# Expert outputs of a pair side by side: one 0/1 product over 128 slots for two over 64, and the expert stage of a hybrid encoder layer reordered by pairs of experts

## The reference, cut to what matters

```python
def _hier_moe(h, router_group, router_expert, e_gate, e_up, e_down):
    ...
    combine = jnp.sum(jax.nn.one_hot(expert_ids, N_EXPERTS, dtype=f32) * w_top[..., None], axis=1).astype(h.dtype)
    out = jnp.zeros_like(ht)
    for e in range(N_EXPERTS):
        hid = jax.nn.silu(ht @ e_gate[e]) * (ht @ e_up[e])
        out = out + combine[:, e:e + 1] * (hid @ e_down[e])
    return out.reshape(B, T, D)

def _layer(...):
    ...
    x = x + gt2 * _hier_moe(h2, router_group, router_expert, expert_w_gate, expert_w_up, expert_w_down)
```

## Time and profile before

| | us |
|---|---|
| median of three runs | 1513.69 (1513.60 to 1515.83) |
| the profiled execution, device time | 1509.26 |
| its span in the profile | 1507.5 |
| TensorE busy in the span | 1400.7 (93%) |
| weights' queue (q1), share of 16 engines' span | 49.8%, 285.07 MB |

### The profile page before, as it was taken

How to read it: one execution, slowest core, us unless ns; L and a number is a source line. 1 busy time by engine, 2 the same in 40 slices (tenths; PEclk the granted TensorE clock), 3 DMA queues, 4 the chain that set the end, 5 groups by cost and what they waited for, 6 DMA issues and landing times. The chain is left out here.

```text
span 1507.5 us, 31643 instructions
## 1 busy us (share of the span) xinstructions
PE 1400.7 (93%) x14017; PEld 1015.6 (67%) x14017; DVE 722.2 (48%) x1184; ACT 473.9 (31%) x764; POOL 167.2 (11%) x200
## 2 busy tenths in 40 slices
PE   5899999999999998888879999799999999999986
PEld 1778999999998987777779998653333333333332
DVE  3322134652235456556555666624555554554545
ACT  2333345554554543333335442110100110011002
POOL 2000000010112124324201101000000000000000
PEclk9999999999999998999999999789999999999988
DMA  8656422234432210000422461499999999999951
GB/s 313 195 187 222 139 72 71 83 110 130 124 90 60 68 44 11 4 5 4 135 56 74 163 213 63 198 407 426 427 426 427 425 427 426 427 426 425 426 232 61
DMA packets 124510, 310.01 MB, mean 206 GB/s; under 512 B 12407, under 2 KB 97617, under 8 KB 109010
## 3 DMA queue, kind: packets, MB, share of 16 engines
q1 hardware_dynamic: 113680, 285.07, 49.8%
q10 hardware_dynamic: 7522, 15.57, 2.9%
q0 software_dynamic: 3168, 7.30, 1.3%
HBM read 299.06 MB, written 12.79 MB: 207 GB/s over the span
## 5 line engine op out<-in xcount | busy, mean ns | idle before, releaser
L838 PE MATMUL bank<-upper2end 128*128 128x272 f32 x3168 | 419.2, 291 | 5.4 <-DVE upper2end L1079 5.4
L838 PEld LDWEIGHTS bank<-upper2end 128*128 128x128 f32 x3168 | 403.4, 189 | 27.5 <-issue 26.2
L1056 DVE TENSOR_TENSOR upper2end<-upper,upper2end 128x1024 fp32r<-128x1024 f32 x66 | 81.7, 1238 | 286.3 <-ACT upper2end L604 286.2
L2711 PE MATMUL bank<-upper7b 128*64 128x512 f32 x784 | 208.0, 603 | 1.0 <-DVE upper7b L3058 1.0
L2491 ACT ACTIVATE upper_r7b<-lower 128x512 fp32r<-128x512 f32 x30 | 18.9, 629 | 407.4 <-DVE lower L3084 407.4
L3111 DVE TENSOR_TENSOR lower<-lower,bank 128x1024 f32<-128x1024 f32 (+1 forms) x75 | 91.4, 1218 | 97.2 <-PE bank L2689 97.2
L2711 PEld LDWEIGHTS bank<-upper7b 128*64 128x64 f32 x784 | 57.7, 137 | 96.9 <-issue 93.0
L2689 PEld LDWEIGHTS bank<-upper_r7b 64*128 64x128 f32 x600 | 52.5, 191 | 86.5 <-DVE lower L3111 58.6
L2689 PE MATMUL bank<-upper_r7b 64*128 64x512 f32 x600 | 93.2, 430 | 18.0 <-DVE lower L3111 9.6
L2543 PE MATMUL bank<-upper_r 128*128 128x272 f32 x768 | 103.0, 294 | 3.2 <-DVE upper_r L2958 3.2
L2543 PEld LDWEIGHTS bank<-upper_r 128*128 128x128 f32 x768 | 99.4, 191 | 5.9 <-DVE upper_r L2790 3.6
(11 more groups left out here) (412 smaller groups left out, 1904.0 us busy)
## 6 DMA issues: line engine op xcount, KB each, us to landing
upper7b<-in_expert_w_gate SPq DMA_DIRECT2D x25, 2048.0 KB, 20.3
upper7b<-in_expert_w_up SPq DMA_DIRECT2D x24, 2048.0 KB, 21.9
upper7b<-in_expert_w_down SPq DMA_DIRECT2D x23, 2048.0 KB, 17.0
upper<-in_w_in SPq DMA_DIRECT2D x66, 512.0 KB, 3.9
lower<-in_w_ada SPq DMA_DIRECT2D x23, 1024.0 KB, 5.0
lower<-in_expert_w_down SPq DMA_DIRECT2D x9, 2048.0 KB, 16.3
lower<-in_expert_w_up SPq DMA_DIRECT2D x8, 2048.0 KB, 23.3
lower<-in_expert_w_gate SPq DMA_DIRECT2D x7, 2048.0 KB, 20.8
```

The costliest lines, as they stand in the source:

```text
L838: m = mm(psum[s][:, c, 0:HALF], w_part[s][:, k, :], h_part[:, k, c * HALF:(c + 1) * HALF], start=k == 0 and w_part is w_high and h_part is ...
L1056: ve.tensor_tensor(w_rest[u % 2], w_slot[u % 2], w_high[u % 2].bitcast(F32), ALU.subtract).then_inc(w_split, 1)
L2711: m = nc.tensor.matmul(psum[s][64 * b:64 * b + 64, 1, :], x_t[(e // 2) % 2][:, k, s * BLK:(s + 1) * BLK], w[:, k, :], start=k == 0, stop=k ...
```

## The change

Both experts of a pair get their `down` in one call: the two experts stand in the two column halves of the array, over four blocks `f` and two output halves `b`, and fill both banks of `psum[2]` with 128 slots by 1024. So scale, rounding and rest become one instruction of 1024 columns for a pair in place of two of 512, and a tile of rows takes 2 parts x 2 halves = 4 products that contract over 128 partitions. The 0/1 matrix is one of 128 slots by 544 rows for a pair; its last 96 columns are zeroed once.

The order on TensorE becomes, for pair p: `gate_up(2p)` with tiles 0 and 1 of pair p - 1 before step 6; `gate_up(2p + 1)` with the turning of expert 2p and tiles 2 and 3 before step 3; `rows_turned(p + 1)`; the turning of expert 2p + 1; tile 4; `down(p)`. `STREAM` takes the matching order. PSUM is dealt anew: gate and up results in banks 0 and 2, turned results in bank 3, turned rows in banks 6 and 7, tiles in `psum[2]`, `psum[3]`, `psum[2]`, `psum[3]`, `psum[0]`. The transposed rows have one buffer, not two. The modulation's gate rows are fetched in full width to all 128 partitions, 2 x 512 KB in place of 4 x 128 KB. The last pair's outputs are now split as all others, by halves of 512. The turning of the first pair's rows, in banks 6 and 7, now waits until the code rows have been copied out of these banks (`code_out`).

```diff
-        act_g = low.take(4, BLK)
-        hid = low.take(4, BLK)
-        gu = [Region(pos_oh_at + 512 * s).take(512) for s in range(2)]
+        hid = [low.take(4, BLK) for _ in range(2)]
...
-        oh_t = moe_r.take(2, 5, P)
-        y_parts = [[moe_r.take(512) for _ in range(2)] for _ in range(2)]
...
+        oh_t = moe_r.take(5 * P)
+        y_parts = [moe_r.take(D) for _ in range(2)]
...
-        STREAM = [("gate", 0), ("up", 0)]
-        for e in range(NE):
-            STREAM += [("gate", e + 1), ("up", e + 1)] * (e + 1 < NE) + [("down", e)]
+        STREAM = []
+        for e in range(0, NE, 2):
+            STREAM += [("gate", e), ("up", e), ("gate", e + 1), ("up", e + 1), ("down", e), ("down", e + 1)]
...
+        GU_BANK = (bank(0), bank(2))
+        TURNED = bank(3)
+        X_BANK = (bank(6), bank(7))
+        ADD_BANKS = (2, 3, 2, 3, 0)
+        LAST_BANKS = (0, 3, 1, 2, 0)
...
+                    sp.dma_start(gt2_b[:, s, :], mod_dram[s, 5 * D:6 * D].partition_broadcast(P)
+                                 ).then_inc(last_rows_in, 16)
...
+                    coef_of_prompt(r, 0)
+                    for p in range(NP):
+                        silu(r, 2 * p)
+                        silu(r, 2 * p + 1)
+                        if p < P_LAST:
+                            y_rounded(r, p)
+                            coef_of_prompt(r, p + 1)
+                    for b in range(2):
+                        last_rounded(r, b)
...
+                    if p == 0 and first(r):
+                        pe.wait_ge(code_out, 4)
...
+                        if h == 0 and p >= 2:
+                            pe.wait_ge(moe_added, r * ADDS + (5 * p - 6))
...
+                    pe.wait_ge(*landed(r, "gate", e))
+                    pe.wait_ge(*landed(r, "up", e))
...
-                    elif not first(r):
...
+                        if s == 0 and p >= 2:
+                            pe.wait_ge(moe_added, r * ADDS + (5 * p - 5))
...
+                        if s == 0 and k == 6 and p:
+                            rows_added(r, p - 1, 0)
+                            rows_added(r, p - 1, 1)
+                        if s == 1 and k == 3:
+                            turned(r, e - 1)
+                            if p:
+                                rows_added(r, p - 1, 2)
+                                rows_added(r, p - 1, 3)
                         for b, w in enumerate(gate_and_up):
...
+                def down(r, p):
+                    pe.wait_ge(hid_done, r * NE + (2 * p + 2))
+                    for s in range(2):
+                        pe.wait_ge(*landed(r, "down", 2 * p + s))
+                    if p:
+                        pe.wait_ge(moe_added, r * ADDS + (5 * p - 2))
+                    w = [weights_of("down", 2 * p + s) for s in range(2)]
                     for f in range(4):
                         for b in range(2):
...
+                            for s in range(2):
+                                m = nc.tensor.matmul(psum[2][64 * s:64 * s + 64, b, :], hid[s][:, f, :],
+                                                     w[s][:, f, b * 512:(b + 1) * 512], start=f == 0, stop=f == 3)
                     m.then_inc(dn_mm, 1)
...
+                def rows_added(r, p, j):
+                    if j == 0:
+                        pe.wait_ge(yrest_done, r * Y_STEPS + (p + 1))
+                        pe.wait_ge(oh_done, r * NP + (p + 1))
+                    if j == 1:
+                        pe.wait_ge(x_t9, r * NE + (2 * p + 4))
+                    if j in (2, 3):
+                        pe.wait_ge(moe_added, r * ADDS + (5 * p + j - 1))
+                    if j == 4:
+                        pe.wait_ge(gu_out, r * NE + (2 * p + 3))
+                    out = psum[ADD_BANKS[j]]
+                    for part in range(2):
+                        for b in range(2):
+                            m = nc.tensor.matmul(out[:, b, :], oh_t[:, j * P:(j + 1) * P],
+                                                 y_parts[part][:, b * 512:(b + 1) * 512], start=part == 0,
+                                                 stop=part == 1)
+                    m.then_inc(moe_mm, 1)
...
+                def last_rows_added(r, j):
+                    if j == 0:
+                        pe.wait_ge(oh_done, r * NP + NP)
+                        pe.wait_ge(moe_added, r * ADDS + ADDS)
                     if j == 4:
                         pe.wait_ge(x3_done, r * 5 + 1)
...
+                    for part, ready in enumerate((yh_done, yrest_done)):
+                        for b in range(2):
+                            if j == 0:
+                                pe.wait_ge(ready, r * Y_STEPS + (P_LAST + b + 1))
+                            m = nc.tensor.matmul(psum[LAST_BANKS[j]][:, b, :], oh_t[:, j * P:(j + 1) * P],
+                                                 y_parts[part][:, b * 512:(b + 1) * 512], start=part == 0,
+                                                 stop=part == 1)
+                    m.then_inc(last_mm, 1)
...
+                    for p in range(NP):
+                        gate_up(r, 2 * p)
+                        gate_up(r, 2 * p + 1)
+                        if p < P_LAST:
+                            rows_turned(r, p + 1)
+                        turned(r, 2 * p + 1)
+                        if p:
+                            rows_added(r, p - 1, 4)
+                        down(r, p)
+                    for j in range(5):
+                        last_rows_added(r, j)
...
+                        ve.memset(oh_t[:, T:5 * P].bitcast(F32), 0.0).then_inc(oh_pad, 1)
+                        v.wait_ge(oh_pad, 1)
...
+                    ve.tensor_scalar(oh_t[:, 0:T], code_rows[0], tgt[:, p:p + 1], None, ALU.is_equal).then_inc(oh_half, 1)
+                    v.wait_ge(oh_half, r * NP + (p + 1))
+                    ve.scalar_tensor_tensor(out=oh_t[:, 0:T], in0=code_rows[1], scalar=tgt[:, p:p + 1],
+                                            in1=oh_t[:, 0:T].bitcast(F32), op0=ALU.is_equal, op1=ALU.add
+                                            ).then_inc(oh_done, 1)
...
+                def down_scaled(r, p):
+                    v.wait_ge(dn_mm, r * NP + (p + 1))
+                    v.wait_ge(coef_done, r * NP + (p + 1))
+                    ve.tensor_tensor(y_full, psum[2].rearrange("t b c -> t (b c)"), coef, ALU.mult).then_inc(y_done, 1)
+                    v.wait_ge(yh_done, r * Y_STEPS + (p + 1))
+                    ve.tensor_tensor(y_parts[1], y_full, y_parts[0].bitcast(F32), ALU.subtract).then_inc(yrest_done, 1)
+
+                def last_scaled(r):
+                    v.wait_ge(dn_mm, r * NP + NP)
+                    v.wait_ge(coef_done, r * NP + NP)
+                    for b in range(2):
+                        half = slice(512 * b, 512 * b + 512)
+                        ve.tensor_tensor(y_full[:, half], psum[2][:, b, :], coef[:, half], ALU.mult).then_inc(y_done, 1)
+                    for b in range(2):
+                        half = slice(512 * b, 512 * b + 512)
+                        v.wait_ge(yh_done, r * Y_STEPS + (P_LAST + b + 1))
+                        ve.tensor_tensor(y_parts[1][:, half], y_full[:, half], y_parts[0][:, half].bitcast(F32),
...
+                    for p in range(NP):
+                        if p:
+                            rows_summed(r, p - 1, 0)
+                            rows_summed(r, p - 1, 1)
+                        gate_up_copied(r, 2 * p)
+                        hidden(r, 2 * p)
+                        if p:
+                            rows_summed(r, p - 1, 2)
+                            rows_summed(r, p - 1, 3)
+                        gate_up_copied(r, 2 * p + 1)
+                        if p < P_LAST:
+                            rows_copied(r, p + 1)
+                        hidden(r, 2 * p + 1)
+                        if p:
+                            rows_summed(r, p - 1, 4)
+                        coef_of_both(r, p)
+                        one_hots(r, p)
+                        if p < P_LAST:
+                            down_scaled(r, p)
```

More of the change, by code:

```diff
@@ L2023, in load_unit, with landed @@
             kind, e = STREAM[n]
-            source, landed = {"gate": (egate, wg_in), "up": (eup, wg_in), "down": (edown, wd_in)}[kind]
-            sp.dma_start(weights_of(kind, e), source[e]).then_inc(landed[e % 3], 16)
+            source = {"gate": egate, "up": eup, "down": edown}[kind]
+            sp.dma_start(weights_of(kind, e), source[e]).then_inc(unit_in[n % 8], 16)
+        def landed(r, kind, e):
+            n = unit_no[kind, e]
+            return unit_in[n % 8], r * (16 * UNIT_USES) + 16 * (n // 8) + 16
         yr_free = sem("yr_free")
```

289 lines of the change are left out of this document (92 added, 197 removed).

## The result

The changed kernel takes **1491.28 us** (median of four runs, 1490.38 to 1493.27) against 1514.39 for the kernel before (four runs): a ratio of 0.985, 95% interval 0.983 to 0.987, or 23.1 us less. The forecast was 1494.8 us, its range 1488 to 1501. The profiled execution took 1490.38 us with a span of 1488.6.

A forecast was written before the change was run, and what follows sets the result against it. TensorE bounds the kernel at 30.68 us a pair, the weight stream close behind at 30.38. Last unit 1457.3, last down 1466.9, plus 3.7, 17.6 and 0.4: span 1488.6, 18.9 less; time 1494.8 us, range 1488 to 1501.

The forecast's parts named there:

- The bound and its change: Expert stage: TensorE sets the pace before; after some five pairs it waits for weights, 10 to 16 us in sum.
- A pair's work: TensorE's work for one pair of experts after the change: 29.0 us (27.1 to 29.9), 1.7 less than before.
- The start: First turning of rows 1.9 us later; first gate_up at 995.1, pair 0 takes 23.9 us, to 1019.0.
- The lead over the stream: At gate_up(2), TensorE's weights landed 7 us ahead; this shrinks 1.4 us a pair, gone after some five.
- The stream: DMA of weights: 30.38 us for a pair's six units, rate unchanged; last unit lands at 1457.3.
- +1.2 us: Gate rows in full width add 512 KB to the weights' queue, delaying the last unit by 1.2 us.
- The end: After the last unit: last down done at 1466.9, then 3.7 us to the first add and 17.6 unchanged.
- The sum: Span 1488.6 us, 18.9 less than 1507.5; taken from the median 1513.7, this gives 1494.8 us.
- Headroom in the stream: Rival: the queue carries faster when asked, so 29.0 us a pair holds to the end; 1481.9 us, chance 0.07.
- Dear products: Rival: a product over 128 partitions costs 0.43 us, a pair 32.9; 1540.4 us, slower than before; chance 0.05.
- The clock's case: Rival: TensorE's clock falls in waits; a 14 us stretch in the last pair costs 6.3 us: 1501.1; chance 0.11.
- The figure that the forecast sets against the trace: The skill's about 358 GB/s a core: a unit would take 6.0 us, the last land 88 us later; measured landings exclude it.

The follow-up runs named there:

- e6: The changed kernel with every unit of weights from the ninth on loading only half of its bytes; 1468.92 us.
- e7: The kernel before the change with every unit of weights from the ninth on loading only half of its bytes; 1513.19 us, ratio 1.000.
- e5: The changed kernel with each tile product of 128 slots split into two over 64 partitions, side by side; 1491.05 us.
- e9: The changed kernel with its five tiles in places of their own again and each 128-slot product split into two over 64 partitions; 1492.94 us.
- e1: The changed kernel without the rests' products, ten of a pair's twenty, in all pairs but the last; 1487.69 us.

## Why the prediction was right

**The bound and its change: right.** TensorE alone for the first pairs, the stream from the sixth interval on, waits of 14.5 us (10 to 16), at the `gate_up` of both experts: the 7.5 us named "issue" at the first, the 7.0 for DMA at the second. The weak point of the reasoning was that before's trace never shows the stream waited for; e6 and e7 show it now.

**A pair's work: right in kind, 0.8 us too high.** Forecast 29.0 (27.1 to 29.9), measured 28.19. Read from the rows of the pair above and their two neighbours: couples with their switches 21.1 (20.6), twenty products with entries and returns 2.05 + 2.01 + 1.17 = 5.2 (5.7), turnings 1.9 (2.5; where three steps stand in one place they share their entry and return), waiting of `down` 0 (0.2). As the text said, the value within its bounds did not matter.

**The start: 1.4 us too early.** The first pair was forecast to be done, and `gate_up(2)` to begin, at 1019.0, that is 57.3 us after the first issue; it began at 1024.3, 58.7 after. The first `gate_up` came 0.5 us earlier than forecast by that measure, but the pair took 25.8 us and not 23.9. The granted clock is 0.57 from 998 to 1002, where before had 1.00 in its first `gate_up`, and the first 44 records take 11.3 us, some 1.7 more than at the full clock (an estimate from the 7.09 us of 32). The waiting, 0.9 us, was as put down (0.8). All this had no effect on the end. The lead over the stream was 10.0 us (forecast 7.3) and shrank by 2.0 a pair (forecast 1.4), so that the stream was met after five pairs as forecast: two misses that cancelled.

**The stream: 3.4 us too slow, in two terms.** Forecast for the last landing were 495.6 us after the first issue, measured 492.2. One term was the gate rows' **"+1.2 us", which was 0**: it counted bytes alone, and the four narrow requests that the change removes had cost as much as the two wide ones that it brings. The other 2.2 us: units 8 to 96 took 445.6 us in before and 443.5 now. Among the nine profiles in which the stream was the bound with whole units, the two with products over 64 partitions (e5, e9) have 445.7 and 445.8, the other seven 443.4 to 443.7; before, whose products are over 64 as well, has 445.6. What those products do to the stream stays open.

**The end: 0.5 us too high.** From the last landing to the end 30.8 (forecast 31.3). Last `down` 1460.5 to 1467.6 (1460.0 to 1466.9), 3.3 us on to the first add (3.7). The clock of the last windows was full, so the 0.4 us for it fell away.

**The sum.** The two misses, 3.4 and 0.5, are 3.9 us of the stage: 22.8 saved and not 18.9. In the profiled execution the span came out at 1488.6, the very figure forecast, because the unchanged code ahead took 3.9 us longer in that execution. In the median that luck is absent, and the forecast was 3.5 us too high. An agreement of spans to the tenth was two errors that cancelled.

**The rivals.** Headroom in the stream fell: 426 GB/s and 30.2 us a pair with TensorE waiting. Dear products fell: 0.22 to 0.26 us. The clock's case came in small: in the window 1320 to 1350 the granted clock is 0.94, after a wait of 2.0 us; the piece of `gate_up` behind that wait took 4.40 us and takes 2.79 elsewhere:

```profile
1328.41 4.40 PE L2721 MATMUL bank<-upper7b 128*64 128x512 f32 x12 [1.97 <-DMA upper7b<-in_expert_w_up]
```

Those 1.6 us came out of the next wait (the pair behind it took 28.75), as the text had it, and in the last pair the clock held.

**The page against the trace.** The figure that the forecast sets against the trace is the table's, the share of a core when both cores of a pair stream. Below it the same section, the Trainium skill, "HBM Reference", Specifications (TRN2), gives about 425 GB/s for a core that streams alone, and the 426 to 428 here agree with that.

## What to carry to other kernels

When two resources are both nearly full, cost a change against the second one first: here 0.3 us a pair was all that separated them, TensorE got 2.5 us a pair cheaper, and of that it could gain no more than its lag behind the stream. Then look where that lag arose. At the last `gate_up` it was 24.3 us more than now, and the slower pace had made only 4.9 of it; the last pair, with its tiles in a row ahead of that `gate_up`, made 15.4. Compare the stage from a fixed event in it, not spans or medians, when the code ahead varies by 7.6 us. And ask of a transfer how many partitions it writes as well as how many bytes.

## What the hardware showed beyond what was expected

- Requests that write 64 partitions ran the sixteen DMA engines at 214 to 287 GB/s, four slices of five at 214 to 227, with a busy share of eights and nines; 512 KB of them delayed the stream by 3.2 us (one run).
- A wait of 2.0 us on TensorE was followed by some 3 us at the lower clock at 1329 us, while other waits of up to 1.6 us in the stage were followed by none. In `e1` a wait of 2.6 us at 1222 was followed by such a stretch, and waits of 2.0, 2.2 and 2.4 us were not: the length of the wait alone does not decide.
- The same code ahead of the stage took 960.5 to 968.1 us in thirteen executions.
- Two products over 64 partitions side by side cost TensorE what one over 128 does: 2.04 us for sixteen, 2.05 for eight.
